# Six merge-gate products moved between the level loop and the attention, a third data row for the position bias, a compressed softmax by two pairs, and another order of the first loads

## What is computed

```python
def compress(k, pos, w1, w2):
    B, G, T, dh = k.shape
    c = k.reshape(B, G, T // CMP_STRIDE, CMP_STRIDE, dh)
    blocks = jnp.concatenate([c[:, :, :-1], c[:, :, 1:]], axis=3) + pos
    flat = blocks.reshape(B, G, blocks.shape[2], CMP_BLK * dh)
    return jax.nn.gelu(flat @ w1) @ w2
...
    y_nsa = nsa_attention(q, kc, vc, ks, vs, kw, vw, gates)
    g = jax.nn.sigmoid(mgate).reshape(B, T, N_BRANCH, D_MODEL)
    m = (g[:, :, 0] * (y_hg @ w_br_hg) + g[:, :, 1] * (y_gla @ w_br_gla)
         + g[:, :, 2] * (y_nsa @ w_br_nsa))
    return m @ w_out
```

## Time and profile before

| what | us |
|---|---|
| median of three executions | 3466.35 (3459.43 to 3467.61) |
| the profiled execution, and its span | 3461.91, 3460.1 |
| TensorE busy | 3310.2 (96%) |
| POOL, DVE, ACT busy | 1856.5 (54%), 1407.5 (41%), 725.0 (21%) |
| level loop's end to the attention's start, layer 0 | 71.40 |
| six gate products and eight spreads of merge 0 | 40.83 |

### The profile page before, as it was taken

The page is one execution under the profiler, slowest core; times in us unless marked ns, Lnnn a source line. Parts: engine busy times, 40 slices in busy tenths (PEclk is TensorE's granted clock), DMA queues, the critical chain, the costliest instruction groups (busy, mean ns, idle before and its releaser), DMA issues.

```text
span 3460.1 us, 43641 instructions
## 1 busy us (share of the span) xinstructions
PE 3310.2 (96%) x15368; PEld 2560.1 (74%) x15368; DVE 1407.5 (41%) x2518; ACT 725.0 (21%) x1482; POOL 1856.5 (54%) x856
## 2 busy tenths in 40 slices
PE   6999999989999999988999999999998899999998
PEld 5678888768888788764766888878877466688886
DVE  4554430455540325845113444132485611244411
ACT  3321000331000223417101110022341710111001
POOL 3257777427777773010445777777300034577774
PEclk8999999999999999968999999999996899999998
DMA  2122222203223222110222322222211012232231
GB/s 107 49 78 94 92 96 92 73 31 106 95 93 97 85 86 67 44 37 1 67 79 86 99 97 91 97 85 88 70 41 43 1 61 79 86 100 96 91 97 61
DMA packets 71438, 263.02 MB, mean 76 GB/s; under 512 B 7920, under 2 KB 7920, under 8 KB 71152
## 3 DMA queue, kind: packets, MB, share of 16 engines
q1 hardware_dynamic: 71280, 260.98, 23.0%
HBM read 258.85 MB, written 2.10 MB: 75 GB/s over the span
## 4 chain that ended last, share of the span: by engine, by line
PE 63%; POOL 15%; issue 14%; DVE 5%; ACT 2%; POOLq 0%; DVEq 0%; DMA 0%; SPq 0%; ACTq 0%
PE bank L565 61%; POOL w_hi L1238 9%; POOL w_lo L1244 6%; PE bank L1129 1%; ACT arena L1662 1%; DVE arena L1705 1%; DVE arena L2221 1%; DVE rope L1702 0%; DVE arena L1702 0%; ACT arena L1651 0%; DVE arena L2061 0%; DVE rope L1705 0%; DVE rope L2281 0%; ACT act_hi L1368 0%; DVE h_lo L1729 0%
## 5 line engine op out<-in xcount | busy, mean ns | idle before, releaser
L1238 POOL TENSOR_TENSOR w_hi<-ring,cst 128x1024 fp32r<-128x1024 f32 x418 | 795.9, 1904 | 1512.2 <-PE bank L565 935.8
L1244 POOL TENSOR_TENSOR w_lo<-ring,w_hi 128x1024 fp32r<-128x1024 f32 x410 | 1016.1, 2478 | 32.2
L565 PE MATMUL bank<-h_hi,w_hi 128*128 128x512 f32 x2256 | 909.2, 403 | 2.1 <-DVE h_lo L1729 2.1
L565 PE MATMUL bank<-h_lo,w_hi 128*128 128x512 f32 x2256 | 894.1, 396 | 0.0
L565 PE MATMUL bank<-h_hi,w_lo 128*128 128x512 f32 x2256 | 889.3, 394 | 0.0
L565 PE MATMUL bank<-act_hi,w_hi 128*128 128x512 f32 (+1 forms) x1296 | 488.2, 407 | 17.7 <-DVE act_lo L1939 8.7
L565 PEld LDWEIGHTS bank<-h_hi,w_hi 128*128 128x128 f32 x2256 | 421.9, 187 | 108.5 <-issue 4.6
L565 PEld LDWEIGHTS bank<-h_hi,w_lo 128*128 128x128 f32 x2256 | 425.4, 189 | 102.7
L565 PEld LDWEIGHTS bank<-h_lo,w_hi 128*128 128x128 f32 x2256 | 424.4, 188 | 97.2 <-issue 1.4
L565 PE MATMUL bank<-act_hi,w_lo 128*128 (+1 forms) x1056 | 423.6, 401 | 0.0
L565 PE MATMUL bank<-act_lo,w_hi 128*128 (+1 forms) x816 | 323.5, 396 | 0.0
(11 more groups left out here) (230 smaller groups left out, 3012.7 us busy)
## 6 DMA issues: line engine op xcount, KB each, us to landing
ring<-wstream SPq DMA_DIRECT2D x480, 512.0 KB, 3.4
par<-params SPq DMA_DIRECT2D x5, 656.5 KB, 4.4
x<-xT SPq DMA_DIRECT2D x4, 512.0 KB, 6.3
outT<-h SPq DMA_DIRECT2D x4, 512.0 KB, 2.7
cst<-const SPq DMA_DIRECT2D x1, 1436.5 KB, 10.4
arena<-pos SPq DMA_DIRECT2D x1, 256.0 KB, 10.4
```

The costliest lines, as they stand in the source:

```text
L565: return pe.matmul(out, lhsT, rhs, start=start, stop=stop)
L1238: return po.tensor_tensor(out, a, C("ones")[:, 0:1].broadcast_to([P, n]), ALU.mult)
L1244: po.tensor_tensor(pair_[1], raw, pair_[0].bitcast(F32), ALU.subtract).then_inc(done.sem, 1)
```

## The change

In both layers of the second block the six gate products of merge 0 leave the merge and are issued by `early_gate` between rotations, hidden products, scores and turns, into banks 6 and 7. Their tiles, in the stream's order 39, 42 and 45 to 48 (the hidden tiles are 40, 41, 43, 44), are split by ACT and DVE as tiles 29 to 38 are; ACT copies each bank to `sig0` and takes the sigmoids behind the last attention output. The position becomes a third row of the data (`cmp_rows`), so that a hidden product has 93 columns and its bias falls out as one of them. The rotations are spread over four banks, the value projection is done four times into groups of 32 rows so that `cmpT` has the heads in row groups, scores come by pair, and DVE's softmax is cut in `cmp_shift` and `cmp_norm`, with ropes and halves between them. The spreads move into and behind the last attention rounds (banks 2 to 5). At the start, positions, 49 columns of constants, parameters and x come first on SP's queue, the remaining 1.4 MB of tables are issued from ACT's queue, POOL has a column of ones of its own, and DVE makes the rotary angles ahead of its part of the front.

```diff
+COLUMNS = slice(CONST["invcount"].start, NCONST)
+TABLES = slice(0, CONST["invcount"].start)
...
-                           ("nv", (NT, 256)), ("gate", (NT, 24)), ("hid", (124,)), ("kc", (62,)), ("vc", (128,)),
+                           ("nv", (NT, 256)), ("gate", (NT, 24)), ("hid", (126,)), ("kc", (62,)), ("vc", (128,)),
...
+        cmp_rows = view(2048, 3, 2 * T)
+        m2["ck"], m2["cv"] = cmp_rows[:, :, 0:T], cmp_rows[:, :, T:2 * T]
...
+        m2["cmpT"] = view(10240, 2, T)
+        m2["sig0"] = view(11264, 6, T)
...
+        EARLY = 6
+        OWN = ZS + EARLY - BY_SCALAR
+        GATE_TILE = (39, 42, 45, 46, 47, 48)
+        HIDDEN_TILE = (40, 41, 43, 44)
...
+        for t in range(39, 49):
+            FREE2.append((ch_mm, HIDDEN_TILE.index(t) + 1) if t in HIDDEN_TILE else
+                         (w2_l, 2 * (ZS - BY_SCALAR + GATE_TILE.index(t)) + 2))
+        FREE2 += [(br_mm, k) for k in (2, 4, 6)]
...
+            sp.dma_start(m1["ta"].bitcast(I32), pos).then_inc(s_pos, 16)
+            sp.dma_start(cst[:, COLUMNS], const[:, COLUMNS]).then_inc(s_pos, 16)
...
-            sp.dma_start(cst[:, :], const).then_inc(s_const, 16)
-            sp.dma_start(m1["ta"].bitcast(I32), pos).then_inc(s_pos, 16)
...
+                    if i >= 4:
+                        pe.wait_ge(*rp_p(l, 2 * (i - 4) + 1))
+                    if i == 3:
+                        pe.wait_ge(*lo_o(l, 8))
+                    product(rotation_bank(i)[:, :], C("rot2"), raw_block(i)).then_inc(rp_mm.sem, 1)
...
-                        product(bank[b1][:, 0:2 * NCMP], w, data[:, :, 2 * p:2 * p + 16 * (NCMP - 1) + 1:16],
-                                p == 0, p == 15)
-                        last = product(bank[b2][:, 0:1], w, par[:, PAR2[posn]][:, p:p + 1], p == 0, p == 15)
...
+                        last = product(b[:, 0:3 * NCMP], ring[:, t % RING, (p % 8) * P:(p % 8) * P + P],
+                                       data[:, :, 2 * p:2 * p + 16 * (NCMP - 1) + 1:16], p == 0, p == 15)
...
+                def early_gate(r, blocks=range(ND)):
+                    if 0 in blocks:
+                        pe.wait_ge(*split_done(l, ZS + r))
+                        if r >= 2:
+                            pe.wait_ge(*mg_c(l, r - 1))
+                        elif r == 1:
+                            pe.wait_ge(*lo_o(l, 7))
+                    for k in blocks:
+                        last = halves_product(bank[6 + r % 2][:, :], r % 2, k, h_hi[:, k, :], h_lo[:, k, :],
+                                              k == 0, k == ND - 1)
+                    if ND - 1 in blocks:
+                        last.then_inc(mg_mm.sem, 1)
...
                 rotation(0)
                 rotation(1)
+                rotation(2)
                 for head, _, _ in LIN[-1][4]:
                     lin_sum(l, head)
                 pe.wait_ge(*ln_st(l, 80))
-                for n in range(4):
-                    hidden(n)
-                    rotation(n + 2)
+                early_gate(0)
+                rotation(3)
+                hidden(0)
+                hidden(1)
+                rotation(4)
+                early_gate(1)
...
+                for i in range(4):
+                    for g in range(2):
+                        last = product(bank[5][32 * i:32 * i + 32, g * 64:g * 64 + 64], m2["hid"][:, 62 + g * 31:94 + g * 31],
+                                       par[:, PAR2["w2_v"]])
...
+                hidden(2)
+                hidden(3)
+                rotation(5)
                 rotation(6)
-                pe.wait_ge(*rp_p(l, 13))
-                pe.wait_ge(*ch_g(l, 1))
-                for g in range(2):
-                    last = product(bank[1][0:NCMP, g * 64:g * 64 + 64], m2["hid"][:, 62 + g * 31:93 + g * 31],
-                                   par[:, PAR2["w2_v"]])
-                last.then_inc(cc_mm.sem, 1)
+                early_gate(2, range(4))
...
+                early_gate(2, range(4, ND))
...
+                pe.wait_ge(*rp_o(l, 8))
                 cmp_scores(0)
                 cmp_scores(1)
...
+                early_gate(3)
+                early_gate(4, range(4))
+                cmp_turn(0)
+                cmp_scores(2)
+                cmp_turn(1)
+                cmp_scores(3)
+                early_gate(4, range(4, ND))
+                early_gate(5)
+                cmp_turn(2)
+                cmp_turn(3)
+                pe.wait_ge(*mg_c(l, EARLY))
+                pe.wait_ge(*rp_o(l, 16))
...
+                    if w == 9:
+                        pe.wait_ge(*ns_m(l, 32))
+                        pe.wait_ge(*lo_rc(l, 1))
+                        for hd in range(4):
+                            lin_spread(hd)
...
+                for hd in range(4, 8):
+                    lin_spread(hd)
...
+                pe.wait_ge(*no_y(l, 4))
+                pe.wait_ge(*lo_n(l, 8))
+                merge_branches(0)
                 with pe.Fori(1, 4) as it:
-                    merge(it)
-                w_out(l + LAYERS, l, lambda l, k: w2_split(l, BY_SCALAR + 24 + k), m_hi, wo_lo, range(ND))
+                    merge_gates(it)
+                    merge_branches(it)
...
+                return po.tensor_tensor(out, a, one.broadcast_to([P, n]), ALU.mult)
...
-                split(ZS)
-                split(ZS + 1)
                 with po.Fori(0, 3) as it:
-                    for s in range(ZS + 2, ZS + 8):
+                    for s in range(ZS + 6, ZS + 12):
...
-            po.wait_ge(s_const, 16)
             po.sem_inc(w_split.sem, w_split.start)
+            po.memset(one[:, :], 1.0).then_inc(s_one, 1)
+            po.wait_ge(s_one, 1)
...
+                    if tables and j == 2:
+                        sc.dma_start(cst[:, TABLES], const[:, TABLES]).then_inc(s_const, 16)
...
+                def gate_copy(r):
+                    sc.wait_ge(*mg_mm(l, r + 1))
+                    sc.activation(m2["sig0"][:, r, :], bank[6 + r % 2][:, :], ACT.Copy).then_inc(mg_c.sem, 1)
...
+                gate_copy(0)
+                cmp_hidden(0)
+                high(12, 0)
+                high(12, 1)
+                gate_copy(1)
...
+                cmp_hidden(1)
+                high(13, 0)
+                high(13, 1)
...
+                gate_copy(2)
+                cmp_exp(0)
+                cmp_exp(1)
+                high(14, 0)
+                high(14, 1)
+                gate_copy(3)
+                for hd in range(2):
+                    cmp_copy(hd)
+                high(15, 0)
+                high(15, 1)
+                for hd in range(2, 4):
+                    cmp_copy(hd)
+                cmp_exp(2)
+                gate_copy(4)
+                cmp_exp(3)
+                gate_copy(5)
...
+                for r in range(EARLY):
+                    sc.wait_ge(*mg_c(l, r + 1))
+                    sc.activation(m2["sig0"][:, r, :], m2["sig0"][:, r, :], ACT.Sigmoid).then_inc(mg_s.sem, 1)
...
+                rope(0)
+                lows(11)
+                for i in range(1, 5):
+                    rope(i)
+                ve.wait_ge(*lo_sd(l, 1))
+                ve.reciprocal(lo_rstd, lo_std).then_inc(lo_rc.sem, 1)
+                ve.memset(mask[:, 0:3 * P], 0.0).then_inc(ns_z.sem, 1)
+                ve.tensor_copy(mask[:, 3 * P:4 * P], C("negdiag")).then_inc(ns_z.sem, 1)
+                lows(12)
+                rope(5)
+                lows(13)
+                cmp_shift(0)
+                cmp_shift(1)
+                rope(6)
+                cmp_norm(0)
+                lows(14)
+                cmp_norm(1)
+                cmp_shift(2)
+                lows(15)
+                cmp_shift(3)
+                cmp_norm(2)
+                cmp_norm(3)
...
+            ve.wait_ge(s_pos, 32)
...
+            for j in range(ND):
+                front((0, j))
+            ve.memset(ksl[:, :, :], 0.0)
+            ve.wait_ge(s_const, 16)
```

253 lines of the change are left out of this document (131 added, 122 removed).

## The result

The changed kernel takes 3365.47 us (median of four, 3362.36 to 3372.69), the kernel before 3463.38 beside it (four, 3459.43 to 3467.61). The ratio is 0.972, with a 95% interval of 0.9698 to 0.9742: 98 us faster, where the forecast was 3384, some 80 faster. The profiled execution took 3362.36 us, with a span of 3360.3.

A forecast was written before the change was run, and what follows sets the result against it. TensorE, busy 96% of the span, bounds the kernel by its work at the granted clock plus few gaps. Twice -33.1 per layer (-66) and -16 at the start make -82, forecast 3384 us on the median, range 3353 to 3420.

The forecast's parts named there:

- Start, -16: Kernel start: reordered loads bring the first norm statistics from 51.53 to 38.5, gain 13.0, plus 3 from the clock.
- rival D: Kernel start: the tables queue behind all ring loads, so the start gains 7 at most less; 3391, chance 0.05.
- Work in the stage, 62.9: Between level loop and attention, per layer: TensorE's work including six gate products, as if all at 2.4 GHz, 62.9 us.
- Gaps, 6.6: Same stage, per layer: TensorE waits 2.9 ahead of gate 4, 2.5 behind gate 5, 1.2 at the first hidden product.
- Clock, +5: Each layer: gaps of 2 to 3 us remain, so one shortened fall to half clock costs 5 us.
- Attention, -3: Attention's first three rounds, per layer: if the clock arrives high they get 3 us shorter, from 33.55.
- Merge, -34.2 and +1: Merge, per layer: six gate products leave, gain 34.2; DVE's last gate-norm steps ahead of the branches, partly uncovered, cost 1.
- The shared port: Stage's last two norms: POOL's weight splits would delay a norm about 2 us per layer, -78 instead of -82; left in range.
- B: Stage between level loop and attention: DVE's order sets the pace, +10 per layer; 3404, chance 0.14.
- C: Same stage: the clock stays low between gates, light work takes twice its time; 3444, chance 0.08.
- F: Same stage: gates raise no clock and run at 1.2 GHz themselves, +27 per layer; 3504, chance 0.02.
- E: Better than the sum: no clock fall, attention 6 instead of 3, start's clock in full, gaps of 3; 3358, chance 0.08.

The follow-up runs named there:

- front_first: Changed kernel with DVE's part of the first front ahead of most of the rotary angles instead of behind them; 3379.82 us.
- before_wide: Kernel before with only the hidden products changed, one 93-column product for each pair, third row being whatever data lies behind; 3440.78 us, ratio 0.992.
- gate5_split: Changed kernel with the sixth gate product moved from the stage into the attention's second round, in two parts of 12 matmuls; 3352.61 us, ratio 0.9669.
- pairs: Changed kernel with the hidden products again as pairs of 62 columns and one column, 32 pairs per layer; 3398.69 us.
- wide_twice: Changed kernel with every 93-column hidden product issued twice, the second into a bank nobody reads; 3394.07 us.

## Why the prediction was right, step by step

**Start, -16.** Measured 17.0. The first product was forecast at 19.7 and came at 19.78, the statistics at 38.5 and 38.81, the clock's share was forecast at 3 and is 12.47 x 0.50 = 6.2 less 12.19 x 0.28 = 3.4, so 2.8. Together that is 15.5, which is the lead of 15.4 at 94.83; the rest of the 17.0 comes later. The tables shared the DMA engines with the ring as supposed: rival D fell. What the steps didn't see is how narrow this was: "they now run ahead of POOL's first split" carried 9 us, as front_first showed, and the last angle step, beside POOL, already took 2.00. That this term came out is in part luck.

**Work in the stage, 62.9.** Measured 62.71 busy, of which some 1.7 are the clock (4.00 us at 0.57). A hidden product takes 5.10 / 16 = 0.32 (forecast 0.30), a gate 5.7.

**Gaps, 6.6.** This term was mis-sized: 2.80. DVE's chain ahead of gate 4 was right (forecast 8.3 to 8.6, measured 8.3 from 1507.30 to 1515.6), but gate 3 ran into the fall of the clock, so that the gap was 1.03 and not 2.9. So 1.7 of the 3.8 us that this term was off only moved out of the gap into a slower product: the fall cost nothing where TensorE would have waited for DVE anyway. Behind gate 5 it was 1.20 and not 2.5, and the first hidden product, forecast at 1.2, waited for nothing: with gate 0 in front, the value copies had 6 us. The 0.57 ahead of the second scores was not in the forecast. I carried gaps over from a stage without cover into one with cover.

**Clock, +5.** Mis-sized as well: one fall of some 4 us, 1.7. The reason I gave for falls, gaps of 2 to 3 us, was the wrong one for this stage: the one fall stands behind a gap of 0.57 (which of what ran ahead of it brought it is not shown). What kept the clock at one half through the hidden products before was their narrow pairs, and those go with the third row; the low clock over the scores and turns stays in before_wide (0.51 from 1518 to 1548), with their gaps. The prediction priced the row as 0.85 against 0.30 at once and so had the sum, but put all of the clock down to the gates: a right number for a reason that is half right. The parts, with 34.2 us of gates counted in: before 105.6, with the third row alone 91.4 (-14.2), with the softmax by pairs, more banks and the gates behind it 83.5 (-7.9), with the gates between 65.5 (-18.0). Of the 7.9, up to 5.5 can be POOL's two splits, which before_wide still has beside DVE's ropes; no run takes them out alone. Of the last step 12.3 are gaps and 5.7 the clock.

**Attention, -3.** Measured 1.3 (32.21 against 33.55). The first rounds are slow because of the gaps of 4.22 and 1.55 in them, which wait for DVE's and ACT's first softmaxes, and the falls of the clock there, although the attention now starts at 1.00; gate5_split shows it by filling both gaps.

**Merge, -34.2 and +1.** The gates went in full, the wait ahead of the branches is 1.06. The spreads cost 3.76 + 3.84 = 7.6 in place of 6.6, about 1 us that I had at nothing.

Per layer -33.1 was forecast and -39.2 and -39.6 measured: 3.8 from the gaps, 3.3 from the clock, less 1.7 in the attention and 1 at the spreads, makes 4.4; the rest, 1.7, is the 1.9 by which TensorE's work in the stage, taken at the full clock, came out under 62.9.

**The shared port.** I had written that POOL is idle in the stage as it was, and that with the change its next splits fall into the last two norms. It is the other way round. Before, two splits ran in the stage (1512.35 to 1516.92 and 1521.09 to 1525.47), where DVE mostly waited for TensorE; now POOL is idle until 1645.37, behind the attention. So the step from DVE's queue to POOL's was argued, not looked up, and the rule had nothing to act on there. At the start it does: 1.42 us against 5.10 for the same two steps, which have two SBUF inputs each, and in before_wide 0.69 against 2.77. There the Trainium skill (GPSIMD Engine Reference, 1. Specifications) and the runs agree. But steps with one SBUF input slow down too (L2423, 0.43 against 2.00), and it is from such a step, L2278, that the forecast took its price; two SBUF inputs don't explain these. That row of the Trainium skill (GPSIMD Engine Reference, 1. Specifications) also names a two-port mode of DVE, and no run here shows whether they ran in it. The front's L1820, one of whose inputs is a PSUM bank, stayed at 0.69 beside the splits.

**Rivals.** B: TensorE waits 2.80 us in all for DVE and ACT, and another order of DVE gets 1.3 back, so DVE doesn't set the pace. (The forecast's terms for DVE's work there add up to 42.2 us, not 44, which changes nothing.) C and F: the clock is 0.97 in the stage, where F needed under 0.58; with the pairs left in (run pairs) C would have come part of the way. E had the direction, but not the reason in the attention. G: the six groups of 24 matmuls stand in the stage where the order puts them.

## What to carry to other kernels

Put dense work that is ready between light work that waits, in pieces of the size of the gaps, and look for the clock's falls behind each gap: the same product was worth 4 us per layer in one piece and 8 in two. Narrow products cost more than their own time where they bring the clock down, so fold a one-column product into its neighbour's columns. And before elementwise work is moved, see which engine runs beside it at the new place.

## What the runs showed of the hardware

A stretch of back-to-back matmuls without any gap brought the granted clock from 1.00 to one half, that is from 2.4 to 1.2 GHz, when the products had 62 columns and one column by turns (run pairs, 0.50 from 1488 to 1492), and the same number of products of 93 columns didn't (run wide_twice, 1.00). In before_wide the clock rose again under wide products and the rotations between them (0.50 before 1504, 1.00 from 1508 to 1514). DVE steps with two SBUF inputs took 2.55 us each beside POOL's splits and 0.71 alone; a step with one SBUF input 2.00 and 0.43. The time from a table load's issue to its landing, 9.2 us beside the ring's loads, was no longer than the 10.4 that a load of nearly the same size had on SP's queue ahead of them.
